# A transformer chain on one core: the projection by tokens made of three rounded products

## The chip, the core and the metric
The kernel runs on one core of a Trainium2 chip. The metric is the time on the device in microseconds (us) of one execution, a median over several. A core has TensorE (matrix products, with weight loads that overlap them), VectorE, ScalarE, GpSimd, and SyncE, which issues most transfers. Products are accumulated in PSUM, in eight banks of 128 partitions by 512 columns of float32.

## The reference, cut to what matters
512 tokens with 1024 channels pass through four layers in float32: two of a first kind (one loop body, run twice), an "even" and an "odd" one. Each begins alike:

```
h = rms_norm(x, pre_mix_w[l])
u = h @ w_in[l]          # then split into parts for convolution, attention, delta rule ...
```

Most columns of `u` are wanted with channels on the partitions. A few are wanted with tokens on the partitions: 408 in each layer of the first kind (the attention's values and the delta rule's gates), 512 in the even layer (half of the gated unit's input), 280 in the odd one (values and gates). Behind come the mixers, an output projection, and a feed-forward (in the odd layer a mixture of experts).

## The kernel before, in words
Activations lie as 8 channel tiles of 128 partitions by 512 tokens (`KD = 8`, `SEQ = 512`, `TT = 4` token tiles). The work is a sequence of phases, written out by hand. `phase` opens semaphores of its own, gives each engine its list of instructions, and closes with a barrier of all engines; nothing crosses it. Every engine works through its list in order and waits only on semaphores.

`rms_norm` leaves the normed stream in `mem.h` and has loaded the weights `w_tm` for the token-major projection; at its end TensorE runs filler products, whose results nobody reads (`fill_in`, L239).

`token_major` (L633) then multiplies: for each token tile and each channel tile the stream's 128 x 128 piece stands in the array and the weights' 408, 512 or 280 columns move (L647). These are products in full float32. ScalarE copies each finished bank out (L660). Beside it `Primer` readies the phase to come: SyncE loads two units of its weights into `weight_ring`, ScalarE rounds the first to `w_high[:, 0]` (L223), VectorE writes the remainder to `w_low[:, 0]` (L230).

`project` (L603) takes SBUF for the parts of its source and calls `linear` (L409), the general dense layer. There a product of float32 matrices is made of three products of rounded parts (type fp32r): high by high, high by low, low by high (L501 to L503). Weights come in units of two output tiles, 16 pieces of 128 x 128, through two slots: load (L472), round on ScalarE (L518), remainder on VectorE (L561), products, copy out (L622). With `source` given, the phase first has to split the stream: ScalarE rounds eight tiles (L554), VectorE takes eight remainders (L597), and TensorE runs five fillers and then, in the first tile of each even unit, waits for the remainders one by one. With `source=None` the parts are there already and there are no fillers. With `primed=SPLIT`, slot 0 is ready: ScalarE and VectorE only mark it so with semaphore increments (VectorE's is L591).

`split_ring` holds `mem.w_high` and `mem.w_low`, 2 slots of 2048 columns. `parts_of` only reserves SBUF. The callers are `second_even`, `second_odd` and `first_block`; in the last two `w_tm` is a buffer of its own.

Of the kernel before, what the change touches and what calls it, by code (L numbers as in the profile page):

```python
# [12 lines left out]
ACT = mybir.ActivationFunctionType  # L13
ALU = mybir.AluOpType
# [3 lines left out]
P = 128  # L18
# [145 lines left out]
@contextmanager  # L164
def phase(nc, *names):


    sems = [nc.alloc_semaphore(f"{n}_{nc.next_id()}") for n in names]
    with nc.Block() as block:
        yield (block, *sems)  # L170
    nc.clear_and_free_semaphores(sems)
    nc.all_engine_barrier()  # L172


@contextmanager
def buffers(nc, **shapes):

    with ExitStack() as stack:
        yield [stack.enter_context(nc.sbuf_tensor(f"{n}_{nc.next_id()}", s, F32)) for n, s in shapes.items()]
# [55 lines left out]
def fill_in(nc, mem, bank, n):  # L235

    tile = mem.filler[:, :]
    for _ in range(n):
        nc.tensor.matmul(bank[:, :], tile, tile.unsqueeze(1).broadcast_to([P, SEQ // P, P]), start=True, stop=True)  # L239
# [363 lines left out]
def project(nc, mem, w, source, evacuate, on_vector=False, primed=0):  # L603

    with parts_of(nc, w.kt) as parts:
        linear(nc, mem, w, parts, evacuate, on_vector, source=source, primed=primed)
# [12 lines left out]
def copy_out(nc, out):  # L619

    def evacuate(bank, tile):
        return nc.scalar.activation(tile_at(out, tile), bank[:, :], ACT.Copy)  # L622
    return evacuate
# [6 lines left out]
    return evacuate  # L630


def token_major(nc, mem, w, cols, source, out, following):  # L633


    with phase(nc, "product", "taken", *Primer.SEMS) as (block, product, taken, *primer_sems):
        primer = Primer(nc, mem, following, primer_sems)

        @block.sync
        def _(sp):  # L640
            primer.load(sp)

        @block.tensor
        def _(pe):
            for t in range(TT):
                for k in range(KD):
                    last = nc.tensor.matmul(mem.bank[t][:, 0:cols], source[:, k, t * P:(t + 1) * P],  # L647
                                            w[:, k * cols:(k + 1) * cols], start=(k == 0), stop=(k == KD - 1))
                last.then_inc(product, 1)

        @block.vector
        def _(dve):
            primer.low(dve)

        @block.scalar
        def _(act):
            primer.high(act)
            for t in range(TT):
                act.wait_ge(product, t + 1)
                nc.scalar.activation(out[:, t, 0:cols], mem.bank[t][:, 0:cols], ACT.Copy).then_inc(taken, 1)  # L660
            act.wait_ge(taken, TT)

class FeedForward:
# [1546 lines left out]
def second_even(nc, mem, a):  # L2212
    with buffers(nc, vec=[P, VECE.size]) as (vec,):
        with buffers(nc, y=[P, KD, SEQ], u=[P, UTE, SEQ], gates=[P, 3, RW_PAIRS, SEQ]) as (y, u, gates):
            decay, rate, gate = [gates[:, i, :, :] for i in range(3)]

            w_tm = gates[:, :, :, :].rearrange("p i j s -> p (i j s)")[:, 0:KD * A_WIDTH]

            pv = y[:, A_GROUPS:KD, :].rearrange("p t n -> p (t n)").rearrange("p (t n) -> p t n", n=A_WIDTH)
            with split_ring(nc, mem):  # L2220
                w_in = Weights(unit_of(a["w_ine"]), UTE // 2, 2, KD)
                rms_norm(nc, mem, mem.x, lambda k: VECE(vec, "norm_mix", k), mem.h,
                         vectors=[(vec[:, :], a["vece"])], ahead=[(w_tm, a["w_tme"])])
                token_major(nc, mem, w_tm, A_WIDTH, mem.h, pv, w_in)
                project(nc, mem, w_in, mem.h, copy_out(nc, u), primed=SPLIT)
            spatial_gate(nc, mem, a, vec, u, pv, y, decay, rate, gate)
            w_out = Weights(unit_of(a["w_oute"]), KD // 2, 2, KD)
            time_mix(nc, mem, vec, u, y, decay, rate, gate, w_out)
            with split_ring(nc, mem):
                project(nc, mem, w_out, y, add_out(nc, mem.x), on_vector=True, primed=LOADED)  # L2230
        ff = FeedForward(unit_of(a["w_ffe"]), unit_of(a["w_downe"]), FFN_T, "silu")
        with split_ring(nc, mem):
            rms_norm(nc, mem, mem.x, lambda k: VECE(vec, "norm_ffn", k), mem.h, following=ff.up[0])
            feed_forward(nc, mem, ff, lambda half: add_out(nc, mem.x), lambda half: True)
# [551 lines left out]
def second_odd(nc, mem, a, out):  # L2786
    with buffers(nc, vec=[P, VECO.size]) as (vec,):
        with buffers(nc, y=[P, KD, SEQ], u=[P, UTO, SEQ], tm=[P, TT, TMO], rope=[P, 2, SEQ], k_cmp=[P, C_KV, N_CMP],
                     v_cmp=[P, C_KV, HEAD]) as (y, u, tm, rope, k_cmp, v_cmp):
            with split_ring(nc, mem):  # L2790
                w_in = Weights(unit_of(a["w_ino"]), UTO // 2, 2, KD)
                with buffers(nc, w_tm=[P, KD * TMO]) as (w_tm,):
                    rms_norm(nc, mem, mem.x, lambda k: VECO(vec, "norm_mix", k), mem.h,
                             vectors=[(vec[:, :], a["veco"])],
                             ahead=[(w_tm[:, :], a["w_tmo"]), (rope[:, :, :], a["rope"])])
                    token_major(nc, mem, w_tm, TMO, mem.h, tm, w_in)
                project(nc, mem, w_in, mem.h, copy_out(nc, u), primed=SPLIT)
            w_out = Weights(unit_of(a["w_outo"]), KD // 2, 2, KD)
            compress(nc, mem, a, vec, rope, u, y, k_cmp, v_cmp, w_out)
            sparse_attention(nc, mem, rope, u, tm, k_cmp, v_cmp, y)  # L2800
            with split_ring(nc, mem):
                project(nc, mem, w_out, y, add_out(nc, mem.x), on_vector=True, primed=LOADED)
        mixture(nc, mem, a, lambda k: VECO(vec, "norm_ffn", k))
        rms_norm(nc, mem, mem.x, lambda k: VECO(vec, "final", k), mem.h, store=out)
# [509 lines left out]
def layer_of(array, l):  # L3314

    one = array[bass.ds(l, 1)]
    names = "abcdefg"[:len(one.shape) - 1]
    return one.rearrange(f"z {' '.join(names)} -> (z {names[0]}) {' '.join(names[1:])}")
# [11 lines left out]
def first_block(nc, mem, a):  # L3330
    with nc.Fori(0, DEPTH) as l, buffers(nc, vec=[P, VEC1.size]) as (vec,):
        with buffers(nc, y=[P, KD, SEQ], u=[P, UT1, SEQ], tm=[P, TT, TM1],
                     lam=[P, 4 * DIFF_DIM + 2], gates=[P, 2, 2 * DELTA_HEADS]) as (y, u, tm, lam, gates):
            with split_ring(nc, mem):
                w_in = Weights(unit_of(a["w_in1"], l), UT1 // 2, 2, KD)
                with buffers(nc, w_tm=[P, KD * TM1]) as (w_tm,):
                    rms_norm(nc, mem, mem.x, lambda k: VEC1(vec, "pre_mix", k), mem.h,
                             vectors=[(vec[:, :], layer_of(a["vec1"], l))],
                             ahead=[(w_tm[:, :], layer_of(a["w_tm1"], l)),
                                    (lam[:, :], a["lam"][bass.ds(l, 1), :].partition_broadcast(P)),  # L3340
                                    (gates[:, :, :], a["gates"][bass.ds(l, 1), :, :].partition_broadcast(P))])
                    token_major(nc, mem, w_tm, TM1, mem.h, tm, w_in)
                project(nc, mem, w_in, mem.h, copy_out(nc, u), primed=SPLIT)
            diff_attention(nc, mem, vec, lam, u, tm, y, a["dist"])
            delta_net(nc, mem, vec, gates, u, tm, y)
            with split_ring(nc, mem):
                w_out = Weights(unit_of(a["w_out1"], l), KD // 2, 2, KD)
                mixer_norms(nc, mem, vec, lam, u, y, w_out)
                project(nc, mem, w_out, y, copy_out(nc, mem.h), primed=SPLIT)
        ff = FeedForward(unit_of(a["w_ff1"], l), unit_of(a["w_ff2"], l), D_FF // P, "relu")  # L3350
        with split_ring(nc, mem):
            add_norm(nc, mem, mem.h, lambda k: VEC1(vec, "post_mix", k), mem.x, lambda k: VEC1(vec, "pre_mlp", k), mem.h,
                     following=ff.up[0])

            feed_forward(nc, mem, ff, lambda half: add_out(nc, mem.h) if half else copy_out(nc, mem.h), bool)
        rms_norm(nc, mem, mem.h, lambda k: VEC1(vec, "post_mlp", k), None, add_to=mem.x)
# [152 lines left out]
```

## Time and profile before

| | us |
|---|---|
| Median of 3 runs (lowest, highest) | 4316.92 (4315.79, 4318.95) |
| Profiled execution, whole | 4322.24 |
| Its span, first to last instruction | 4320.4 |
| TensorE busy (share) | 4047.2 (94%) |
| VectorE busy (share) | 1539.7 (36%) |
| ScalarE busy (share) | 1323.6 (31%) |

The profile comes from one execution. A group of instructions is named by the line that issues it, its engine, and output<-inputs. "PEld" is the weight load of TensorE. Products are pipelined: each lasts longer than the distance to the next, and the distance is the pace. "Idle before" names what let the engine go on. The granted clock (PEclk) is a share of 2.4 GHz; 0.5 is 1.2 GHz. Times in the timeline run from the first instruction.

### The profile page before, as it was taken

The numbers are of one execution on the slowest core, as the hardware profiler recorded it, in microseconds if no ns is written. First come the engines' busy times: TensorE is split into PE (matmuls) and PEld (weight loads), VectorE is DVE, ScalarE is ACT, GpSimd is POOL, SyncE is SP. The second block draws the span as 40 slices with busy tenths as digits, with TensorE's granted clock in tenths as the row PEclk, the third lists the DMA queues.
The fourth block names the chain that finished last, engine by engine and source line by source line (L and its number), as shares of the span: only waits on it lengthen the run. The fifth ranks groups of instructions, "written<-read, shape, count | busy, mean of one in ns | idle before, by whom it ended". The sixth has DMA issues, their size and how long they took to land. (4 is left out here: it accounts for less than half of the span.)

```text
span 4320.4 us, 56641 instructions
## 1 busy us (share of the span) xinstructions
PE 4047.2 (94%) x22051; PEld 3372.8 (78%) x22051; DVE 1539.7 (36%) x2719; ACT 1323.6 (31%) x2282; POOL 224.2 (5%) x187
## 2 busy tenths in 40 slices
PE   8999999999999989999998889999998879999999
PEld 5778787787677878678766776877776659999998
DVE  2364544332226554333333654322315421111121
ACT  2364443232237544332223332322223311111111
POOL 0150100000006010000000000000000000000000
PEclk9998989999999888999999889999999789999999
DMA  3100011221210000122211001222221025555544
GB/s 125 44 1 1 0 39 69 89 96 59 76 53 1 1 0 29 69 88 97 68 69 54 1 1 68 91 89 85 82 73 65 15 72 187 204 212 180 217 169 148
DMA packets 54648, 333.49 MB, mean 77 GB/s; under 512 B 7600, under 2 KB 8496, under 8 KB 23520
## 3 DMA queue, kind: packets, MB, share of 16 engines
q1 hardware_dynamic: 51904, 324.95, 21.5%
q0 software_dynamic: 2592, 6.49, 0.6%
q8 instruction: 99, 1.62, 0.2%
q14 instruction: 53, 0.43, 0.0%
HBM read 326.17 MB, written 4.19 MB: 76 GB/s over the span
## 5 line engine op out<-in xcount | busy, mean ns | idle before, releaser
L501 PE MATMUL bank<-high 128*128 128x512 f32 x2480 | 973.5, 393 | 40.8 <-DVEq L591 22.8
L502 PE MATMUL bank<-low,high 128*128 128x512 f32 x2480 | 972.0, 392 | 0.0
L503 PE MATMUL bank<-high,low 128*128 128x512 f32 x2480 | 972.0, 392 | 0.0
L501 PEld LDWEIGHTS bank<-high 128*128 128x128 f32 x2480 | 470.0, 190 | 146.8 <-DVEq L591 25.7
L503 PEld LDWEIGHTS bank<-high,low 128*128 128x128 f32 x2480 | 469.5, 189 | 98.8
L502 PEld LDWEIGHTS bank<-low,high 128*128 128x128 f32 x2480 | 469.6, 189 | 97.3
L561 DVE TENSOR_TENSOR low<-weight_ring,high 128x2048 fp32r<-128x2048 f32 (+1 forms) x144 | 319.3, 2219 | 544.8 <-ACT high L518 544.8
L3137 PE MATMUL bank<-chosen,glu_ring 128*128 128x176 f32 x2816 | 424.6, 313 | 0.0
L3137 PEld LDWEIGHTS bank<-chosen,glu_ring 128*128 128x128 f32 x2816 | 421.5, 191 | 0.0
L518 ACT ACTIVATE high<-weight_ring 128x2048 fp32r<-128x2048 f32 (+1 forms) x144 | 266.6, 1853 | 262.9 <-PE bank L503 229.1
L239 PE MATMUL bank<-filler 128*128 128x512 f32 x1023 | 291.3, 432 | 20.4 <-PEq L172 14.4
L239 PEld LDWEIGHTS bank<-filler 128*128 128x128 f32 x1023 | 204.5, 203 | 83.4 <-issue 32.9
L3151 PE MATMUL bank<-hidden,down_ring 128*128 128x176 f32 x1408 | 211.3, 313 | 0.0
L3151 PEld LDWEIGHTS bank<-hidden,down_ring 128*128 128x128 f32 x1408 | 210.4, 190 | 0.0
L1414 DVE TENSOR_TENSOR joint<-bank,level_masks 128x512 f32<-128x512 f32 x224 | 153.8, 691 | 145.9 <-PE bank L1433 145.9
L741 POOL TENSOR_TENSOR y<-y,scaled 128x512 f32<-128x512 f32 x120 | 149.6, 1274 | 1007.1 <-ACT scaled L775 1007.1
L3259 DVE TENSOR_TENSOR hidden<-silu,bank 128x176 f32<-128x176 f32 x88 | 29.7, 337 | 385.8 <-ACT silu L3215 385.8
L3215 ACT ACTIVATE silu<-bank 128x176 f32<-128x176 f32 x88 | 27.9, 317 | 448.6 <-PE bank L3137 448.6
L569 DVE TENSOR_TENSOR gated<-gated,bank 128x512 f32<-128x512 f32 x86 | 58.9, 685 | 284.8 <-ACT gated L525 158.5
L622 ACT ACTIVATE u<-bank 128x512 f32 (+1 forms) x84 | 50.3, 598 | 332.0 <-PE bank L503 332.0
L1446 PE MATMUL bank<-weight_ring,joint 128*128 128x128 f32 x1152 | 151.8, 276 | 0.0
L1446 PEld LDWEIGHTS bank<-weight_ring,joint 128*128 128x128 f32 x1152 | 139.5, 192 | 0.9
(506 smaller groups left out, 4653.5 us busy)
## 6 DMA issues: line engine op xcount, KB each, us to landing
glu_ring<-in_w_expert SPq DMA_DIRECT2D x88, 1024.0 KB, 5.1
weight_ring<-in_w_ff SPq DMA_DIRECT2D x64, 1024.0 KB, 5.0
down_ring<-in_w_expert_down SPq DMA_DIRECT2D x64, 704.0 KB, 5.0
weight_ring<-in_w_in SPq DMA_DIRECT2D x22, 1024.0 KB, 4.8
weight_ring<-in_w_ffe SPq DMA_DIRECT2D x22, 1024.0 KB, 4.8
weight_ring<-in_w_downe SPq DMA_DIRECT2D x16, 704.0 KB, 4.1
weight_ring<-in_w_ino SPq DMA_DIRECT2D x11, 1024.0 KB, 4.9
weight_ring<-in_w_ine SPq DMA_DIRECT2D x9, 1024.0 KB, 4.9
```

Source lines behind the costliest of these rows:

```text
L239: nc.tensor.matmul(bank[:, :], tile, tile.unsqueeze(1).broadcast_to([P, SEQ // P, P]), start=True, stop=True)
L501: nc.tensor.matmul(mem.bank[b][:, :], whole, high[:, k, :], start=(k == 0), stop=False)
L502: nc.tensor.matmul(mem.bank[b][:, :], whole, low[:, k, :], start=False, stop=False)
L503: last = nc.tensor.matmul(mem.bank[b][:, :], rest, high[:, k, :], start=False, stop=(k == kt - 1))
L518: nc.scalar.activation(w_high[:, s, :], mem.ring[:, s, 0:size], ACT.Copy).then_inc(high_ready[s], 1)
L561: nc.vector.tensor_tensor(w_low[:, s, :], mem.ring[:, s, 0:size], w_high[:, s, :], ALU.subtract).then_inc(low_ready[s], 1)
L569: nc.vector.tensor_tensor(whole, whole, mem.bank[b][:, :], ALU.mult).then_inc(taken[b], 1)
L741: nc.gpsimd.tensor_tensor(y[:, c, :], y[:, c, :], scaled[:, n % CONV_SLOTS, :], ALU.add).then_inc(added, 1)
L1414: nc.vector.tensor_tensor(chunks(joint[:, n, :]), chunks(turn_bank(i)[:, :]), mask, ALU.mult) \
L1446: last = nc.tensor.matmul(product_bank(i)[:, c], joint[:, n, c], matrix[:, n, c], start=True, stop=True)
L3137: last = nc.tensor.matmul(two(low[s])[:, half, :], glu_ring[:, s, at:at + P], chosen[:, k, :], start=(k == 0), stop=(k == KD - 1))
L3151: last = nc.tensor.matmul(two(high[m // 2])[:, m % 2, :], down_ring[:, s, k * P:(k + 1) * P], hidden[:, k, :], start=(k == 0), stop=(k == ...
```

## The change
`token_major` gets two more buffers, the stream's parts, and makes each product of three rounded ones. The loop over channel tiles is now outermost, the one over token tiles inside: the four token tiles accumulate in banks 0 to 3 side by side, with three products each per channel tile. ScalarE rounds the weights' piece and the stream's tile, VectorE takes both remainders, tile by tile. The weights' parts lie in slot 1 of the ring's parts, free in this phase, in four places of `cols` columns each; for channel tiles 4 to 7 ScalarE waits on `used` until TensorE has left the place. TensorE begins with seven fillers into bank 4.

The stream's parts are reserved by the caller and passed on to `linear` directly, without `source`, so it splits nothing and fills nothing. In `second_odd` and `first_block`, `w_tm` now lies in the memory of `y`, which is written only later.

```diff
-def token_major(nc, mem, w, cols, source, out, following):
+def token_major(nc, mem, w, cols, source, parts, out, following):
+    places = KD // 2
+    w_high, w_low = mem.w_high[:, 1, :], mem.w_low[:, 1, :]
+    high, low = parts
...
+        of = [slice(k * cols, (k + 1) * cols) for k in range(KD)]
+        at = [of[k % places] for k in range(KD)]
...
         @block.tensor
         def _(pe):
-            for t in range(TT):
-                for k in range(KD):
-                    last = nc.tensor.matmul(mem.bank[t][:, 0:cols], source[:, k, t * P:(t + 1) * P],
-                                            w[:, k * cols:(k + 1) * cols], start=(k == 0), stop=(k == KD - 1))
-                last.then_inc(product, 1)
+            fill_in(nc, mem, mem.bank[TT], 7)
+            for k in range(KD):
+                pe.wait_ge(w_low_ready, k + 1)
+                pe.wait_ge(low_ready, k + 1)
+                for t in range(TT):
+                    to, tokens = mem.bank[t][:, 0:cols], slice(t * P, (t + 1) * P)
+                    nc.tensor.matmul(to, high[:, k, tokens], w_high[:, at[k]], start=(k == 0), stop=False)
+                    nc.tensor.matmul(to, high[:, k, tokens], w_low[:, at[k]], start=False, stop=False)
+                    last = nc.tensor.matmul(to, low[:, k, tokens], w_high[:, at[k]], start=False, stop=(k == KD - 1))
+                    if k == KD - 1:
+                        last.then_inc(product, 1)
+                if k < KD - places:
+                    last.then_inc(used, 1)
 
         @block.vector
         def _(dve):
+            for k in range(KD):
+                dve.wait_ge(w_high_ready, k + 1)
+                nc.vector.tensor_tensor(w_low[:, at[k]], w[:, of[k]], w_high[:, at[k]], ALU.subtract) \
+                    .then_inc(w_low_ready, 1)
+                dve.wait_ge(high_ready, k + 1)
+                nc.vector.tensor_tensor(low[:, k, :], source[:, k, :], high[:, k, :], ALU.subtract) \
+                    .then_inc(low_ready, 1)
             primer.low(dve)
 
         @block.scalar
         def _(act):
+            for k in range(KD):
+                if k >= places:
+                    act.wait_ge(used, k - places + 1)
+                nc.scalar.activation(w_high[:, at[k]], w[:, of[k]], ACT.Copy).then_inc(w_high_ready, 1)
+                nc.scalar.activation(high[:, k, :], source[:, k, :], ACT.Copy).then_inc(high_ready, 1)
             primer.high(act)
...
@@ second_odd; first_block and second_even alike @@
-                with buffers(nc, w_tm=[P, KD * TMO]) as (w_tm,):
...
-                    token_major(nc, mem, w_tm, TMO, mem.h, tm, w_in)
-                project(nc, mem, w_in, mem.h, copy_out(nc, u), primed=SPLIT)
+                w_tm = y[:, :, :].rearrange("p t n -> p (t n)")[:, 0:KD * TMO]
...
+                with parts_of(nc, KD) as parts:
+                    token_major(nc, mem, w_tm, TMO, mem.h, parts, tm, w_in)
+                    linear(nc, mem, w_in, parts, copy_out(nc, u), primed=SPLIT)
```

## Rows read from the trace of the kernel before

**Rows 1.** The page, part 1: busy us, share of the span, instructions.
```profile
PE 4047.2 (94%) x22051; PEld 3372.8 (78%) x22051; DVE 1539.7 (36%) x2719; ACT 1323.6 (31%) x2282; POOL 224.2 (5%) x187
```

**Rows 2.** Groups by line and form, TensorE: count, busy us, mean ns, idle before.
```profile
L647 PE MATMUL bank<-w_tm,h_branch 128*128 128x408 f32 x128 | 44.3, 507 | 1.6 <-PEq L172 1.6
...
L647 PE MATMUL bank<-gates,h_branch 128*128 128x512 f32 x64 | 27.7, 593 | 0.8 <-PEq L172 0.8
...
L647 PE MATMUL bank<-w_tm,h_branch 128*128 128x280 f32 x64 | 15.3, 400 | 0.8 <-PEq L172 0.8
```

**Rows 3.** Busy time by stretch: stretch, length, TensorE busy (count), clock, DMA share, GB/s.
```profile
35.00:57.50 22.50, 22.16 (x64) 1.00 0.25 94
...
2216.00:2243.90 27.90, 27.70 (x64) 1.00 0.20 76
3096.60:3112.10 15.50, 15.33 (x64) 1.00 0.37 135
...
60.60:64.40 3.80, 3.76 (x10) 0.55 0.62 252
...
2247.20:2260.00 12.80, 12.80 (x57) 1.00 0.41 152
```

**Rows 4.** Timeline, first layer's seam: start us, us (merged), instruction, idle before.
```profile
58.80 1.40 PE L239 MATMUL bank<-filler 128*128 128x512 f32 x5 [1.44 <-PEq L172]
59.14 4.28 ACT L554 ACTIVATE high<-h_branch 128x512 fp32r<-128x512 f32 x8 [1.23 <-PEq L172]
...
59.80 4.91 DVE L597 TENSOR_TENSOR low<-h_branch,high 128x512 fp32r<-128x512 f32 x8 [15.51 <-ACT high L554]
...
60.64 0.56 PE L501 MATMUL bank<-high 128*128 128x512 f32 x1 [0.45 <-DVE low L597]
```

**Rows 5.** One line's instructions, odd dense layer: ns min/median/max, first to last start.
```profile
L622 ACT ACTIVATE u<-bank x22: 597/599/601, 3121.1 to 3235.2; 128x512 f32 x16, 128x512 f32<-128x512 f32 x6
```

**Rows 6.** Timeline, the first dense layer's rounded products.
```profile
61.42 0.63 PE L503 MATMUL bank<-high,low 128*128 128x512 f32 x1
...
64.36 0.40 PE L501 MATMUL bank<-high 128*128 128x512 f32 x1
...
70.94 0.39 PE L503 MATMUL bank<-high,low 128*128 128x512 f32 x1
```

**Rows 7.** Timeline, odd layer's attention: weight loads of two 128-column rounded products.
```profile
3282.22 0.30 PEld L2586 LDWEIGHTS bank<-masked,exact_ident 128*128 128x128 f32 x2
```

**Rows 8.** Groups by line and form, ScalarE: rounding copies of two widths.
```profile
L518 ACT ACTIVATE high<-weight_ring 128x2048 fp32r<-128x2048 f32 x128 | 244.7, 1912 | 178.9 <-PE bank L503 148.3 <-PEq L172 30.6
...
L518 ACT ACTIVATE high<-weight_ring 128x1408 fp32r<-128x1408 f32 x16 | 21.9, 1383 | 84.0 <-PE bank L503 80.8 <-PEq L172 3.2
```

**Rows 9.** Timeline, first token-major stretch: the next layer's preparation and an evacuation.
```profile
40.06 1.91 ACT L223 ACTIVATE high<-weight_ring 128x2048 fp32r<-128x2048 f32 x1 [12.50 <-DMA weight_ring<-in_w_in]
...
41.87 0.49 ACT L660 ACTIVATE tm<-bank 128x408 f32<-128x408 f32 x1
42.00 2.29 DVE L230 TENSOR_TENSOR low<-weight_ring,high 128x2048 fp32r<-128x2048 f32 x1 [9.02 <-ACT high L223]
```

**Rows 10.** Timeline, a seam without fillers inside the feed-forward, TensorE.
```profile
892.53 0.50 PE L501 MATMUL bank<-high 128*128 128x512 f32 x1 [2.22 <-DVEq L591]
...
894.27 0.63 PE L501 MATMUL bank<-high 128*128 128x512 f32 x1
```

**Rows 11.** One line's instructions: VectorE's mark in the first layer's seam.
```profile
L591 DVEq EVENT_SEMAPHORE  x1: 21/21/21, 58.8 to 58.8; - x1
```

**Rows 12.** Timeline, the even layer's seam, TensorE.
```profile
2245.30 1.39 PE L239 MATMUL bank<-filler 128*128 128x512 f32 x5 [1.52 <-PEq L172]
...
2247.14 0.47 PE L501 MATMUL bank<-high 128*128 128x512 f32 x1 [0.45 <-DVE low L597]
```

**Rows 13.** Groups by line and form: 128-column products, full precision (L830), rounded (L2586).
```profile
L830 PE MATMUL bank<-const_cols,probs 128*128 128x128 f32 x384 | 52.5, 282 | 1.4 <-ACT y L767 1.4
...
L2586 PE MATMUL bank<-masked,exact_ident 128*128 128x128 f32 x64 | 14.8, 315 | 0.0
```

More of the change, by code:

```diff
@@ L630, in add_out @@
     return evacuate
-def token_major(nc, mem, w, cols, source, out, following):
-    with phase(nc, "product", "taken", *Primer.SEMS) as (block, product, taken, *primer_sems):
+def token_major(nc, mem, w, cols, source, parts, out, following):
+    places = KD // 2
+    w_high, w_low = mem.w_high[:, 1, :], mem.w_low[:, 1, :]
+    high, low = parts
+    with phase(nc, "w_high_ready", "w_low_ready", "high_ready", "low_ready", "used", "product", "taken", *Primer.SEMS) as (
+            block, w_high_ready, w_low_ready, high_ready, low_ready, used, product, taken, *primer_sems):
         primer = Primer(nc, mem, following, primer_sems)
+        of = [slice(k * cols, (k + 1) * cols) for k in range(KD)]
+        at = [of[k % places] for k in range(KD)]
         @block.sync
@@ L2223, in second_even @@
                          vectors=[(vec[:, :], a["vece"])], ahead=[(w_tm, a["w_tme"])])
-                token_major(nc, mem, w_tm, A_WIDTH, mem.h, pv, w_in)
-                project(nc, mem, w_in, mem.h, copy_out(nc, u), primed=SPLIT)
+                with parts_of(nc, KD) as parts:
+                    token_major(nc, mem, w_tm, A_WIDTH, mem.h, parts, pv, w_in)
+                    linear(nc, mem, w_in, parts, copy_out(nc, u), primed=SPLIT)
             spatial_gate(nc, mem, a, vec, u, pv, y, decay, rate, gate)
@@ L2791, in second_odd @@
                 w_in = Weights(unit_of(a["w_ino"]), UTO // 2, 2, KD)
-                with buffers(nc, w_tm=[P, KD * TMO]) as (w_tm,):
-                    rms_norm(nc, mem, mem.x, lambda k: VECO(vec, "norm_mix", k), mem.h,
-                             vectors=[(vec[:, :], a["veco"])],
-                             ahead=[(w_tm[:, :], a["w_tmo"]), (rope[:, :, :], a["rope"])])
-                    token_major(nc, mem, w_tm, TMO, mem.h, tm, w_in)
-                project(nc, mem, w_in, mem.h, copy_out(nc, u), primed=SPLIT)
+                w_tm = y[:, :, :].rearrange("p t n -> p (t n)")[:, 0:KD * TMO]
+                rms_norm(nc, mem, mem.x, lambda k: VECO(vec, "norm_mix", k), mem.h,
+                         vectors=[(vec[:, :], a["veco"])],
+                         ahead=[(w_tm, a["w_tmo"]), (rope[:, :, :], a["rope"])])
+                with parts_of(nc, KD) as parts:
+                    token_major(nc, mem, w_tm, TMO, mem.h, parts, tm, w_in)
+                    linear(nc, mem, w_in, parts, copy_out(nc, u), primed=SPLIT)
             w_out = Weights(unit_of(a["w_outo"]), KD // 2, 2, KD)
@@ L3335, in first_block @@
                 w_in = Weights(unit_of(a["w_in1"], l), UT1 // 2, 2, KD)
[L3336 to L3343, printed above, removed]
+                w_tm = y[:, :, :].rearrange("p t n -> p (t n)")[:, 0:KD * TM1]
+                rms_norm(nc, mem, mem.x, lambda k: VEC1(vec, "pre_mix", k), mem.h,
+                         vectors=[(vec[:, :], layer_of(a["vec1"], l))],
+                         ahead=[(w_tm, layer_of(a["w_tm1"], l)),
+                                (lam[:, :], a["lam"][bass.ds(l, 1), :].partition_broadcast(P)),
+                                (gates[:, :, :], a["gates"][bass.ds(l, 1), :, :].partition_broadcast(P))])
+                with parts_of(nc, KD) as parts:
+                    token_major(nc, mem, w_tm, TM1, mem.h, parts, tm, w_in)
+                    linear(nc, mem, w_in, parts, copy_out(nc, u), primed=SPLIT)
             diff_attention(nc, mem, vec, lam, u, tm, y, a["dist"])
```

## The prediction
> **What bounds the kernel now.** I read the page's busy shares first: TensorE is busy 94% of a span of 4320.4 us, VectorE 36%, ScalarE 31% [rows 1]. So only what TensorE executes, or waits for, can move the time. The groups by line and form then give the products that the change rewrites: 64 instructions with 408 moving columns in each of two runs of the layer loop, 64 with 512, 64 with 280 [rows 2]. The busy time by stretch shows each of the four stretches filled to the edge by them (22.16, 22.16, 27.70, 15.33 us, together 87.35) at a granted clock of 1.00, that is 2.4 GHz [rows 3]. Last, the timeline shows the seam behind: last product, a 1.44 us gap, five filler products, and only 1.84 us after the first filler the first real product of the dense layer, let go by VectorE's remainder of the stream [rows 4]. All of this is in series on TensorE. The dense layer behind the seam is bound by TensorE too: in the odd block 22 evacuations start from 3121.1 to 3235.2 us, 5.43 us apart, close to 24 products of 0.227 us [rows 5, 6].
>
> **1. The products.** A full-precision product is two instructions here (32 products, 64 instructions). From 280 to 408 columns the 64 instructions gain 6.83 us [rows 3], so a column costs 0.833 ns in one instruction and 1.67 ns in a product. The rounded products of the dense layers are one instruction each and start 0.227 us apart at 512 columns (64.36 to 70.94 over 29 of them [rows 6]); at 0.833/2 = 0.417 ns a column that is 213.3 ns plus 14 ns. After the change there are 32 x 3 = 96 rounded instructions a stretch. No row shows one with 408 or 280 columns. If the 14 ns stays fixed, they come every 0.184 and 0.131 us; if it is proportional, every 0.181 and 0.124. Above, the bound is 0.227 as for 512 columns (something other than columns sets the pace). Could weight loads do that? Two loads for 128-column rounded products take 0.30 us together where one lasts 0.19, so they start 0.11 apart [rows 7]; that is under 0.131. I take 0.184 and 0.131.
>
> The Trainium skill, page "TensorE: Matmul & The Clock Gate", section "Back-to-back issue gap", gives N/2.4 + 2.5 ns, which is 215.8 ns at 512 columns; this trace shows 227, so for this data type the row decides. By the page's figure the four stretches would be another 4.4 us shorter.
>
> **2. The head.** Real products now wait for ScalarE's rounded weights and stream and VectorE's remainders. The seam shows such a chain: first filler 58.80, ScalarE 59.14, VectorE 59.80, product 60.64, so 1.84 us [rows 4]. The new one has a copy of the weights more ahead of the stream's: eight copies of 512 columns take 4.28 us, 0.52 each in a row [rows 4, 8]; with (1912 - 1383)/640 = 0.83 ns a column [rows 8] 0.44 for 408 and 0.33 for 280. The weights' remainder on VectorE lies beside the stream's copy. The first product thus comes 2.28, 2.36 and 2.17 us in (408, 512, 280). The 7 new fillers need about 6 x 0.23 + 0.39 = 1.8 us and hide in it.
>
> **3. Supply.** Per channel tile ScalarE needs 0.44 + 0.52 = 0.96 us and VectorE at most 0.60 + 0.60 = 1.2 (eight remainders in 4.91 us [rows 4]); TensorE needs 12 x 0.184 = 2.2, 1.57 at 280 columns. From tile 4 on ScalarE waits for a place, free when TensorE leaves tile k - 4; three tiles of products (4.7 us at least) then stand between, against 2 us of preparing. Behind that wait on ScalarE queue the next layer's rounding (1.91 us), VectorE's remainder (2.29) and the four evacuations. The tightest is 280 columns: place for tile 7 free at 2.17 + 4 x 1.57 = 8.5, copies done at 9.4, rounding 11.3, remainder 13.7, products done 14.9. Covered; if it were not, up to 2 us would stand open in this one stretch. The ring's loads are issued at the start as before, and used from 40.06, 4.9 us in, in the first stretch [rows 9]. The tail stays: all four banks now end in the last tile, 3 x 0.184 = 0.55 apart, and an evacuation takes 0.49 [rows 9]; after the last product still one is due.
>
> Stretches, first filler to end of last product (a last product lasts its distance plus 0.17):
> - 408: 2.28 + 95 x 0.184 + 0.35 = 20.1, before 22.16: -2.05, twice.
> - 512: 2.36 + 95 x 0.227 + 0.39 = 24.3, before 27.70: -3.4.
> - 280: 2.17 + 95 x 0.131 + 0.30 = 14.9, before 15.33: -0.4.
> Sum -7.9. With 0.181 and 0.124 it is -9.1; with 0.227 throughout it is +9.6 (24.2 twice, 24.1 once).
>
> **4. The seam.** The dense layer now finds both parts. Its 5 fillers, the 16 copies and remainders, and the wait go. What is late next is the mark from VectorE that slot 0 is ready: in the feed-forward's unfilled seams TensorE is let go by just that mark [rows 10]; in our seams it falls with the first filler, at 58.8 [rows 11]. I allow 0.1 us behind it. So 1.84 becomes 0.1: -1.74 at each of four seams (the others have the same 1.84, as the even block's 2245.30 to 2247.14 [rows 12]), -7.0. At the other end, a gap as long as the 2.22 us of [rows 10] leaves 1.44 + 1.84 - 2.22 = 1.06 a seam, 2.7 us less in all. The slot-1 rounding, queued behind the eight stream copies so far, starts 4.3 us earlier and was hidden (unit 0 takes 10.9 us). The eight waits per even unit on the stream's parts also go; the steady 5.43 us of [rows 5] says they cost nothing. Moving the weights into y's buffer changes an address, no instruction.
>
> **Sum.** -7.9 - 7.0 = -14.9 us against the profiled execution's 4322.24 (span 4320.4 plus 1.84 around it): 4307.3. The median of the runs shown is 5.3 us lower, 4316.92, so I forecast **4302 us**.
>
> **Rivals.**
> (a) The clock. In the first layer TensorE fell to 1.2 GHz right behind the seam: products of 0.63 us instead of 0.39, mean clock 0.55 from 60.6 to 64.4 [rows 3, 6]; in the other three seams, equally built, it stayed at 1.00 (the even block's stands for them [rows 3]). A slow stretch of 3.4 us costs 1.7. The seams without fillers inside the feed-forward, gap 2.22 us, do fall (products of 0.63 us behind it [rows 10]). Ours will have a gap of 1.44 + 0.1 without fillers; the even block's 1.52 gap followed by fillers and another 0.45 wait did not fall [rows 3, 12]. If all four seams fall: +5.1, 4307. If all four heads fall too (gap 0.77, fillers, then half a microsecond of waiting): eight stretches for one, +11.9, 4314.
> The Trainium skill, same page, section "The HAM clock gate (the 'warmup' mystery)", says the throttled state is the default and activity lifts it; that speaks against taking out fillers, and the first seam agrees. By it rival (a) is real.
> (b) The pace does not fall with columns: 0.227 everywhere. Then +9.6 - 7.0 = +2.6: 4320, no change. Against it the 0.11 us between loads and the per-column rows; for it only that no row shows the form.
> (c) The other side: rounded products with fewer columns lose the one-pass rate. The rows give it some colour: a 128-column rounded product (L2586) takes 0.315 us in the mean, a full-precision one of the same size (L830) 0.282 in the mean [rows 13], where 512 columns show 0.39 against 0.59 [rows 2, 6]. If 408 and 280 columns ran at full precision's pace per instruction (0.342, 0.236), the stretches would be 35.3 twice and 25.0: +13.1, +13.1, +9.6, with -3.4 and -7.0: +25.5, 4342. It decides from 0.052 us more for each of the 288 instructions with short rows (14.9/288), 0.236 at 408. I doubt it: those are single pairs among other work, and a duration of 0.17 us plus the 0.11 between their loads [rows 7] gives 0.28 whatever the columns do.
>
> **How the numbers follow.** Forecast with its neighbourhood 0.80, (a) in force 0.10, (b) 0.05, (c) 0.04, else 0.01. The forecast's own range is 4294 to 4308: down by 1.2 for the proportional pace, and by 1.7 for each slow stretch elsewhere (the unfilled feed-forward seams among them) that a program 15 us shorter may not meet; up by one to three slow stretches. For 8 in 10 with part of (a): 4293 to 4312. Some 0.2%, 8.6 us, is what a measurement tells from no change; below 4308.3 is faster. Half of (a) and all of the forecast's case are faster: 0.85; same 0.11 (half of (a), (b)); slower 0.04.
>
> **What would show it.** Right: 96 instructions a stretch, 0.184 and 0.131 us apart at clock 1.00; TensorE busy without gaps behind the first real product, 2.2 to 2.4 us after the first filler; a gap of about 1.55 us at the seam and no L597-like remainder there; stretches of 20.1, 24.3, 14.9. Wrong: a distance of 0.227 at 280 columns (b) or above it (c); distances of 0.43 behind the seams (a); TensorE waiting on VectorE between tiles, which would break step 3.

## The result and the profile after

The changed kernel takes 4288.98 us in the median of 11 runs (4283.1 to 4309.83), the kernel before, run beside it, 4318.17 (4307.16 to 4325.53). The ratio is 0.9938, 95% interval 0.9923 to 0.9952: 26.8 us less. Forecast were 4302 us and a gain of 14.9, with a range of 4293 to 4312. The direction was right, the size was not: nearly twice the gain. Two executions, one of run 1 (6186.64 us) and the profiled one of run 9 (6188.29 us), were in a slower state and are left out of every figure below, so that run 9 has no profile.

The profiled execution took 4308.07 us, 14.2 less than that of before, which looks like the forecast's 14.9. First the page of the changed kernel, then the granted clock of this execution and of a second profiled one of the same kernel.

```profile
span 4306.3 us, 57009 instructions
...
PE 4030.0 (94%) x22187; PEld 3386.2 (79%) x22187; DVE 1556.6 (36%) x2751; ACT 1339.6 (31%) x2314; POOL 224.2 (5%) x187
```

```profile
core 0: 4306.3 us, clock 0.948
```

```profile
core 0: 4283.1 us, clock 0.955
```

The same program, 23 us apart, with the shorter time at the higher clock. So one pair of profiles cannot confirm a total, and what has to be read first is what is the same in both. Busy time by stretch of the changed kernel (stretch, length, TensorE busy and count, clock, DMA share, GB/s): the four token-major stretches and the beginnings of the four dense layers, answering to [rows 3].

```profile
35.50:57.50 22.00, 20.02 (x104) 1.00 0.25 96
1130.90:1152.90 22.00, 19.96 (x103) 1.00 0.25 96
2207.20:2233.50 26.30, 23.90 (x103) 1.00 0.22 80
3080.60:3096.80 16.20, 14.38 (x104) 1.00 0.34 130
57.40:70.00 12.60, 12.56 (x48) 0.86 0.46 168
1152.90:1165.00 12.10, 12.09 (x46) 0.86 0.50 175
2233.50:2246.00 12.50, 12.49 (x55) 1.00 0.51 169
3096.80:3110.00 13.20, 13.20 (x58) 1.00 0.47 160
```

The new products, by line and form, against [rows 2]; then the timeline of the first head (the time from the first filler to the first product) and the first seam, against [rows 4]; then VectorE's mark in that seam, against [rows 11].

```profile
L656 PE MATMUL bank<-high 128*128 128x408 f32 x64 | 22.4, 351 | 0.2
...
L656 PE MATMUL bank<-high 128*128 128x512 f32 x32 | 12.5, 391 | 0.2 <-DVE low L671 0.2
...
L656 PE MATMUL bank<-high 128*128 128x280 f32 x32 | 9.4, 294 | 0.0
```

```profile
35.58 1.83 PE L239 MATMUL bank<-filler 128*128 128x512 f32 x7 [0.77 <-PEq L172]
37.49 0.42 PE L656 MATMUL bank<-high 128*128 128x408 f32 x1
...
55.27 0.35 PE L658 MATMUL bank<-high,low 128*128 128x408 f32 x1
57.44 0.47 PE L501 MATMUL bank<-high 128*128 128x512 f32 x1 [1.82 <-DVEq L591]
...
58.49 0.63 PE L502 MATMUL bank<-low,high 128*128 128x512 f32 x1
```

```profile
L591 DVEq EVENT_SEMAPHORE  x1: 21/21/21, 57.1 to 57.1; - x1
```

TensorE's first product starts 1.91 us after its first filler. It runs 96 products 0.187 us apart without a gap, idles 1.82 us and then finds the dense layer ready. From the first filler or product to the dense layer's first product (called a stage below):

| us | first, l=0 | first, l=1 | even | odd | sum |
|---|---|---|---|---|---|
| before | 25.44 | 25.44 | 31.07 | 18.51 | 100.46 |
| after | 21.86 | 21.86 | 26.17 | 16.08 | 85.97 |
| difference | -3.58 | -3.58 | -4.90 | -2.43 | -14.49 |
| forecast | -3.8 | -3.8 | -5.1 | -2.1 | -14.9 |

The second profile of either kernel repeats these to 0.03 us. Behind the first two seams the clock falls (0.86; products of 0.63 us at 58.49), 1.65 us each. In the first profile of before only the first seam's did, in its second profile the first's and the fourth's.

### The profile page after: what moved, and what is told of

It is laid out like the page before. It is cut to its first block and busy times, and to the rows that moved or that the text cites. A ratio compares the mean times of both kernels' runs of the same rounds, so it can differ in the third digit from the quotient of the medians.

```text
span 4306.3 us, 57009 instructions
## 1 busy us (share of the span) xinstructions
PE 4030.0 (94%) x22187; PEld 3386.2 (79%) x22187; DVE 1556.6 (36%) x2751; ACT 1339.6 (31%) x2314; POOL 224.2 (5%) x187
```

## Where the other half is: the granted clock

Each run lists its mean clock. Through all runs of the full kernels whose clock is listed (172, of twelve kernels, each with a level of its own) one common slope fits to 2.1 us: -3659 us per unit of clock. The last column is each kernel's level, read at a clock of 0.950.

| kernel | runs | mean us | mean clock | us at 0.950 by the fit |
|---|---|---|---|---|
| before | 73 | 4321.6 | 0.9472 | 4311.5 |
| before, as a kernel of its own (run 1) | 11 | 4318.1 | 0.9481 | 4311.1 |
| changed | 11 | 4292.8 | 0.9518 | 4299.4 |
| changed, again (2) | 6 | 4292.1 | 0.9522 | 4300.0 |
| products alone (3) | 12 | 4304.6 | 0.9496 | 4303.1 |
| seam alone (4) | 12 | 4311.3 | 0.9487 | 4306.7 |
| before, 6 fillers (5) | 11 | 4317.0 | 0.9494 | 4314.7 |
| changed, 16 fillers (6) | 5 | 4293.2 | 0.9528 | 4303.4 |
| changed, 10 fillers (7) | 5 | 4295.5 | 0.9512 | 4299.9 |
| changed, odd layer 12 (8) | 10 | 4301.0 | 0.9496 | 4299.5 |
| changed, tail fillers (11) | 5 | 4296.0 | 0.9504 | 4297.4 |
| before, 7 fillers (12) | 11 | 4322.1 | 0.9485 | 4316.4 |

At equal clock the change is worth some 12 us; 0.0046 of clock are another 17. The clock column is rounded to 0.001 (3.7 us), so this is a split, not a measurement of either part. Where the time lies is read from the four profiles of the two kernels, the span cut into five kinds of stretches. A mixer's stretch runs from its first TensorE instruction to the first product of the output projection.

| us | up to the first token-major product or filler | token-major and seam, four | dense layers, four | mixers, four | behind the mixers, four |
|---|---|---|---|---|---|
| before | 35.20 | 100.46 | 474.85 | 1369.41 | 2340.51 |
| before, again | 34.95 | 100.45 | 476.46 | 1377.29 | 2333.65 |
| changed | 35.58 | 85.97 | 476.56 | 1367.39 | 2340.79 |
| changed, again | 35.45 | 85.94 | 476.63 | 1351.72 | 2333.31 |

The 14.5 us are in both pairs. The mixers are 2.0 us shorter in the first pair and 25.6 in the second. What lies behind them differs by 7 us between the two profiles of either kernel. In the changed kernel that is the part behind the odd mixer, where the experts run: 877.9 us in the first profile, of these 54.6 at 1.2 GHz, and 869.9 with 37.6 in the second. That the first pair came so near the forecast was luck.

## Experiments

**1 and 2. Both kernels again.** No edit. 

> The kernel before, once more, for its spread and the clock of every run. Theory A (lottery of the clock): the four seam stretches are steps of fixed length; what else moved is time at 1.2 GHz in the mixers, whose amount is drawn anew in every execution. Then plotted against the granted clock the runs lie on one line, us = a - b x clock, with b near 3400 us per unit (the eleven runs of the changed kernel: 4309.8 at 0.947, 4283.1 at 0.955), and the line of the kernel before lies 14.5 us above that of the changed one. Theory B (another part of the change saves more than the seams show): the distance between the lines is 25 us or more. Median expected 4312 to 4322, profiled clock 0.944 to 0.951.

> The changed kernel once more. Theory A: median 4283 to 4300; where its profile has a granted clock above 0.950 the time missing against the first profile (4306.3) lies in the mixers and in the seams' slow stretches alone, while the four token-major stages stay at 21.9, 21.9, 26.2, 16.1 us. Theory B: some stage other than those is shorter than in both earlier profiles at equal time at 1.2 GHz.


Measured: 4318.6 us (ratio to before 0.9991, 0.9976 to 1.0006), profiled clock 0.947; and 4292.34 (0.994, 0.9927 to 0.9954), 0.955. The lines of the fit lie 12 us apart, not 25, so theory B is out. The 23 us between the changed kernel's two profiles are not in the mixers and seams alone, as expected: 15.7 are in the mixers, 8 behind the odd one. The second pass of the first kind's mixer, in the profiles of before (first execution), before again, changed, changed again:

```profile
1277.84:1720.31 442.47, 409.89 (x2847) 0.89 0.02 7
```

```profile
1276.90:1719.90 443.00, 410.83 (x2846) 0.89 0.02 7
```

```profile
1276.58:1712.19 435.61, 403.28 (x2846) 0.91 0.02 7
```

```profile
1269.40:1704.80 435.40, 402.21 (x2846) 0.91 0.02 7
```

Same instructions, 7 us less, at a higher clock, in both profiles of each kernel. Two against two speaks against a draw by chance (theory A as first put), and the mixer's code is untouched.

**3. Products alone.** The changed kernel, but the dense layer splits its source again:
```diff
-                    linear(nc, mem, w_in, parts, copy_out(nc, u), primed=SPLIT)
+                    linear(nc, mem, w_in, parts, copy_out(nc, u), source=mem.h, primed=SPLIT)
```


> The changed token-major phase, but the dense layer behind it splits the stream itself again with its five fillers. Stages token-major plus seam (first filler or product to the dense layer's first product): 1.73 us longer than in the changed kernel at each of four places, so 23.6, 23.6, 27.9, 17.8 us. Theory A: 6.9 us above the changed kernel at equal clock. If the seam's missing fillers cost slow stretches in the changed kernel (two of four seams show one in its first profile, 1.7 us each), the gap in the median is smaller, about 4 us. Theory B puts the surplus of some 12 us in one of the two parts: this kernel then shows it or not.


Measured: 4302.56 us (0.9964, 0.9951 to 0.9976). Stages 23.36, 23.36, 27.53, 17.59: 8.6 us less than before, and the seam's share is 1.4 to 1.5 a piece, not 1.73. No seam falls in clock. The second mixer takes 435.4 us here.

**4. Seam alone.** Full-precision products, the stream's parts made beside them, tile by tile, on ScalarE (shown) and VectorE; the weights are not split:
```diff
         def _(act):
+            for k in range(KD):
+                nc.scalar.activation(high[:, k, :], source[:, k, :], ACT.Copy).then_inc(high_ready, 1)
             primer.high(act)
```


> The full-precision products and their loop order as before; ScalarE and VectorE make the stream's parts beside them, and the dense layer takes them without fillers. Expected -1.74 us at each of four seams: stages of 23.7, 23.7, 29.3, 16.8 us where the kernel before has 25.44, 25.44, 31.07, 18.51. Theory A: 7.0 us below the kernel before at equal clock. Theory B: one of this and the kernel with the products alone shows some 12 us more than that.


Measured: 4308.98 us (0.9979, 0.9963 to 0.9995). Stages 23.96, 23.95, 29.57, 17.01, -1.5 each, -6.0. No seam falls in clock here either, though none has fillers. The second mixer takes 450.9 us; the profiled execution is the slowest of the twelve. The two halves shorten the stages by 8.6 and 6.0, together 14.6, and by their ratios the whole by 15.6 (10.4 to 21.2) and 9.1 us (2.2 to 16.0). Theory B's single culprit is not there. The surplus of the products' half is clear of noise, that of the seam's half is not.

**A sharper theory.** The clock record of each trace lists when the granted clock changed. Within one execution all falls lie on one regular grid of times, to 0.007 us, in all profiles. Where a kernel starts on it differs from run to run, but the first mixer brings all into step: the output projection behind it started 0.42 to 0.83 us behind a grid point in all twelve profiles, wherever the mixer itself had started (from 0.2 to 3.4). From there the lengths in between set where the second mixer starts. I call the time from the last grid point to a mixer's start its offset. A': the offset decides how much of the mixer runs at 1.2 GHz. B': it does not.

**5 to 8. Moving the offset.** Fillers at the head of the token-major phase:
```diff
+            fill_in(nc, mem, mem.bank[TT], pad)      # before: pad=6 (run 5) or 7 (run 12), first kind only
```
```diff
-            fill_in(nc, mem, mem.bank[TT], 7)        # changed: 16 (run 6), 10 (7) in the first kind, 12 (8) in the odd layer
```


> The kernel before with six fillers put ahead of the token-major products in both layers of the first kind: pure extra work, 1.43 us each, TensorE's stage 25.44 -> 26.9 us. Theory A' (the first mixer brings the program into step with the grid of clock changes; where the second layer's mixer then begins on that grid is set by the lengths in between, and so is its time at 1.2 GHz): offset of the second mixer's start from the last change of the clock goes from 1.4-1.8 us to 2.85-3.2, the changed kernel's 3.1-3.2, and the mixer takes about 435.5 us instead of 442.5-443.0. Net 2.9 - 7: faster than the kernel before by some 4 us in the median, though it only does more. Theory B' (the change itself made the second mixer shorter, through addresses or otherwise; the clock is drawn at random): mixer stays 442 to 443, and the kernel is 2.9 us slower.

> The changed kernel with 16 fillers instead of 7 at the head of the token-major phase in the first kind of layer: the first product comes 3.8 us in instead of 1.91, +1.9 us twice. [...] Theory B': +3.8 us only, the mixer stays at 435.5.

> The changed kernel with 10 fillers at the same place, +0.47 us twice. [...] Theory B': +1 us.

> The changed kernel with 12 fillers instead of 7 in the odd layer's token-major phase alone, +0.94 us once. The odd mixer started at offset 2.46 and 2.84 in the changed kernel's profiles (210.2 and 205.3 us), at 0.04 and 0.08 in two others (221.2, 221.1). Theory A': the offset becomes 3.4 to 0.4 and the mixer 213 to 221 us, +5 to +14 us in the median. Theory B': +0.9 us.


Measured: before with 6 fillers 4316.01 us against 4322.73 in its set, but by the ratio only 2.6 us less (0.9994, 0.998 to 1.0008): the interval holds both forecasts, 4 less and 2.9 more. By the fit the 2.8 us of added work are there (4314.7 against 4311.5 at equal clock) and a higher mean clock gave them back. The changed kernel with 16 took 4295.69 (ratio to before 0.9937), with 10 4298.06 (0.995), with 12 in the odd layer 4300.88 (0.9958), against 4292.34 (0.994) without, from 5, 5 and 10 runs whose standard deviation is 4 to 8 us. The medians decide little, so the profiles have to.

There no forecast of A' for a mixer's length came true. Before with 6 fillers reached offset 2.93 as meant, but its second mixer took 441.4 us, not 435.5. A' put that mixer at 442.5 to 443 us with 16 fillers in the changed kernel and at 451 with 10. But 16 fillers took away the slow stretch behind the second seam (1.65 us), so the offset stayed at 3.17 and the mixer at 435.4; 10 fillers gave 3.40 and 441.1. The odd mixer reached offset 3.41 as meant and took 210.8 us, short of the band of 213 to 221.

**9 and 10. No mixers at all.** In both kernels, all mixers are left out; the output projections of the even and odd layer then load their first weights themselves:
```diff
-            diff_attention(nc, mem, vec, lam, u, tm, y, a["dist"])
-            delta_net(nc, mem, vec, gates, u, tm, y)
+            stand_in(nc, mem, y)        # y = mem.h; the even and odd layers' mixers likewise
```


> The kernel before with the mixers left out (attention, delta rule, gated unit and time mix, sparse attention; a copy of the normed stream stands in for their result), everything else kept. The experts may get other token counts than in the full kernel, so only the difference to the next kernel counts. If the surplus over the seams' 14.5 us comes from time at 1.2 GHz in the mixers, the two differ by 12.8 to 14.5 us (14.5 less up to one slow stretch of 1.7) and the spread of either over its runs is under 3 us where the full kernel's is 6 to 9. If the surplus lies outside the mixers, they differ by 20 us or more.

> The changed kernel with the same mixers left out: 12.8 to 14.5 us below the one before it (theory A'), or 20 us and more (theory B').


Measured: 3134.34 us (3132.03 to 3135.58), and 3117.33 (3116.22 to 3121.64). Difference 17.0 in the median, 15.6 in the mean with a standard error of 1.3: above the forecast's 12.8 to 14.5, but not clearly, and far from the full kernels' 26 to 29. The spread is 4 and 5 us, not under 3, but the full kernels' sets of five or six runs spread by 10 to 19.

**11. Tail fillers.** In the changed kernel, work for TensorE while it waits for the last evacuation and the barrier:
```diff
                 if k < KD - places:
                     last.then_inc(used, 1)
+            fill_in(nc, mem, mem.bank[TT], 3)
```


> The changed kernel with three fillers behind the last product of every token-major phase, where TensorE waits for the last evacuation and the barrier. They take 0.7 us of an idle 1.44 us and should cost nothing. The slow stretches behind the first and second seam go: dense layers 123.7 -> 122.05 us twice, -3.3. Theory A' adds that the second mixer then begins 1.65 us earlier on the grid, at 1.5 instead of 3.1-3.2, where the kernel before had it, and takes 442.5 to 443 instead of 435.5: +3.7 in the median over all. Theory B': -3.3.


Measured: 4293.48 us (0.9936, 0.9917 to 0.9956), the changed kernel's within what 5 runs tell; they cannot tell the two forecasts apart. Timeline of the first and of the second seam, then the clock behind them:

```profile
54.28 0.35 PE L658 MATMUL bank<-high,low 128*128 128x408 f32 x1
54.46 0.87 PE L239 MATMUL bank<-filler 128*128 128x512 f32 x3
56.45 0.48 PE L501 MATMUL bank<-high 128*128 128x512 f32 x1 [1.12 <-DVEq L591]
...
1138.49 0.87 PE L239 MATMUL bank<-filler 128*128 128x512 f32 x3
1140.47 0.47 PE L501 MATMUL bank<-high 128*128 128x512 f32 x1 [1.12 <-DVEq L591]
```

```profile
56.40:69.00 12.60, 12.55 (x55) 1.00 0.46 168
1140.50:1152.50 12.00, 12.00 (x53) 1.00 0.50 176
```

The stages stay at 21.86 us, so the fillers are free, and both slow stretches are gone: dense layers 122.10 and 122.05 instead of 123.7. In the second seam that is the fillers' doing: from the last product's end to the dense layer the gap lies 0.39 to 2.21 us behind a grid point here and 0.44 to 2.26 in the changed kernel, where the clock falls. The first seam proves nothing: the gap begins 1.80 us behind a grid point, and the changed kernel without mixers, whose gap begins at 1.65 without fillers, keeps the full clock there as well.

The second mixer, now at offset 1.38, has the length of the kernel before. Here it is cut in six, first this kernel, then the kernel before (offset 1.42), then the changed one (3.22):

```profile
1262.50:1372.50 110.00, 107.90 (x697) 0.94 0.02 5
1372.50:1422.50 50.00, 43.24 (x275) 0.79 0.00 1
1422.50:1502.50 80.00, 76.47 (x574) 0.90 0.01 1
1502.50:1582.50 80.00, 71.49 (x556) 0.94 0.00 0
1582.50:1662.50 80.00, 72.94 (x550) 0.89 0.00 0
1662.50:1705.30 42.80, 38.86 (x203) 0.76 0.14 51
```

```profile
1276.90:1386.90 110.00, 107.84 (x697) 0.94 0.02 5
1386.90:1436.90 50.00, 43.38 (x275) 0.78 0.01 1
1436.90:1516.90 80.00, 76.25 (x573) 0.90 0.00 1
1516.90:1596.90 80.00, 71.53 (x555) 0.94 0.00 0
1596.90:1676.90 80.00, 72.83 (x551) 0.89 0.00 0
1676.90:1719.70 42.80, 39.02 (x206) 0.76 0.16 53
```

```profile
1269.40:1379.40 110.00, 108.21 (x679) 0.92 0.02 5
1379.40:1429.40 50.00, 43.08 (x308) 0.87 0.00 1
1429.40:1509.40 80.00, 71.53 (x565) 0.95 0.00 1
1509.40:1589.40 80.00, 76.36 (x574) 0.90 0.00 0
1589.40:1669.40 80.00, 71.59 (x556) 0.94 0.00 0
1669.40:1704.80 35.40, 31.43 (x177) 0.81 0.17 63
```

Two different kernels with the same offset agree slice by slice to 0.01 of clock; the same kernel but for three free fillers, with another offset, does not. This is A' at its cleanest, forecast before the run (442.5 to 443; it took 442.8). A rival goes with it: that the second mixer got shorter because the change moved buffers. This kernel has every buffer where the changed one has it. By the fit the tail fillers' kernel is 2.0 to 2.6 us faster at equal clock, and a lower mean clock gives that back.

**12. Seven fillers on the kernel before.**


> The kernel before with seven fillers (six brought the second mixer to offset 2.93 and 441.4 us) ahead of the token-major products in the first kind of layer: +1.66 us twice. Theory A': offset 3.15, mixer 435 to 436 us, net -3.5 on the kernel before. Theory B': +3.3.


Measured: 4324.69 us (0.9995, 0.998 to 1.0009), which again holds both forecasts. Offset 3.18 as meant, mixer 441.4 instead of 435 to 436: its clock falls where those of the other mixers at 3.18 do for 324 us, then one slow stretch lasts longer, and the rest differs. So the offset is not all. The second mixers of the full kernels:

```
offset  0.22   1.38   1.42   1.79   2.90   2.93   3.09   3.17   3.18   3.18   3.22   3.40
us     450.9  442.8  443.0  442.5  432.1  441.4  435.6  435.4  435.4  441.4  435.4  441.1
```
(in this order: seam alone; tail fillers; before again; before; changed, odd 12; before + 6; changed; changed, 16; products; before + 7; changed again; changed, 10.) The kernel before sits in the 442 to 443 group, the changed one in the 432 to 436 group. Neighbours mostly agree, but not always: 2.90 and 2.93 are 9 us apart.

The odd mixer shows the limit more plainly. At offsets of 0.04 (seam alone) and 0.09 (before again) it took 221.2 and 221.1 us, at 0.08 (before + 7) 210.9:

```profile
3231.40:3452.50 221.10, 198.38 (x1065) 0.82 0.10 35
```

```profile
3229.65:3440.60 210.95, 187.89 (x1064) 0.86 0.11 37
```

At 2.46 to 2.49 it took 210.2, 210.2, 204.8 and 209.0 us in four versions of the changed kernel.

**13 to 16. Which mixers.** Both kernels with only the first kind's mixers, and with only the even and odd layers' (the edit of 9, in part).


> The kernel before with the mixers of the even and odd layer left out (a copy of the normed stream stands in) and those of the first kind kept. If the surplus is in the second pass of the first kind's mixer, this kernel and the next differ by 14.5 + 7 = 21 to 24 us, and the profiles show that mixer at 442 to 443 here. If it is elsewhere, by 14 to 17.

> The changed kernel with the even and odd mixers left out: 21 to 24 us below the one before it, its second mixer at 432 to 436 us; or 14 to 17 if the surplus lies in the other mixers.

> The kernel before with only the even and the odd mixer kept. If the surplus is the first kind's, this and the next differ by 14 to 17 us; the odd mixer alone may add up to 8 (mean of profiles 216 against 208 us), then 20 to 24.

> The changed kernel with only the even and the odd mixer kept: 14 to 17 us below the one before it, or 20 to 24 with the odd mixer's share.


Measured: 3958.74 and 3935.95 us, 22.8 apart (21.4 in the mean); 3594.26 and 3570.94, 23.3 apart (23.3). Over the 17.0 (15.6) without mixers that is 5.8 for the first kind's and 6.3 for the others' (5.8 and 7.7 in the means). Added up, 29.1: the full kernels' 26 to 29. Second mixer in the first pair, odd mixer in the second, before and after each:

```profile
1275.90:1722.00 446.10, 412.64 (x2846) 0.89 0.02 7
```

```profile
1271.80:1703.90 432.10, 397.76 (x2846) 0.92 0.02 7
```

```profile
2419.20:2630.50 211.30, 188.47 (x1064) 0.86 0.11 36
```

```profile
2399.20:2604.50 205.30, 181.72 (x1064) 0.90 0.11 37
```

The first line is a miss: 442 to 443 us were expected, and at offset 1.68, between two mixers of that length, it took 446.1. The changed kernel's 432.1 us at 2.87 equals the 432.1 at 2.90 above. Five runs each, with standard errors of 1.7 to 2.3 us: 5.8 and 6.3 have standard errors of some 3 us, so that both groups of mixers have a share is likely and not shown.

## Why the prediction was right or wrong

1. **Products.** Right. 0.187 us apart at 408 columns for 0.184, 0.129 at 280 for 0.131; 280 columns last 0.294 where 0.30 was forecast; clock 1.00. Rivals (b) and (c) are out.
2. **Head.** 1.91 us for 2.28. ScalarE begins with TensorE here (35.55), not 0.34 later as at the seam, whose lag I had taken over. It gave back what the pace cost, which is luck.
3. **Supply.** Right. L656 idles at most 0.2 us in either wide form, over two layers at 408 columns. In the odd layer, the tightest case, the next layer's remainder began at 3091.76 and lasted 2.29 us; the last product began at 3094.80.
4. **Seam.** Gap 1.82 for 1.54 us. VectorE's mark came when it should, 1.46 us behind the last product's end (57.08 in the trace); the first product came 0.36 behind the mark, where I had allowed 0.1. -1.5 us a seam, not -1.74, -6.0 for -7.0. The bound of 2.22 was not reached.
5. **Rival (a).** Real, and small where I put it: two seams fall instead of one, +1.65. Heads never fall. But a missing filler alone does not do it: with the seam alone no seam fell. The tail fillers' run bears the rival out in the second seam. The rule cited from the Trainium skill, page "TensorE: Matmul & The Clock Gate", section "The HAM clock gate (the 'warmup' mystery)", that activity lifts the throttled state, agrees with this seam.
6. **The step that failed** is the clock's term in the forecast's own range: "down ... by 1.7 for each slow stretch elsewhere ... that a program 15 us shorter may not meet". I took the rest of the program's time at 1.2 GHz as given, give or take a stretch or two, and carried the profile's distance to the median over. In its place the mixers, which make up a third of the time and run 40 to 113 us each at 1.2 GHz, lose or gain whole groups of slow stretches when they start elsewhere on the grid. That was worth some 12 us here: 26.8 measured for 14.5 in the stages, and 15.6 without mixers. In the profiles 7 of them are the second mixer's (442.5 and 443.0 us before, 435.6 and 435.4 after). The term's size was unknown, not zero, and the range should have been about 12 us wider on either side; the seam change alone shows in its profile that it can as well go up (450.9).

What is shown: the 14.5 us and their places; that some 12 us more need the mixers; that near offsets gave equal second mixers in two different kernels, and another offset another length. Argued only: that the offset carries the mean difference. It came true in one forecast of a mixer's length out of six, the tail fillers', and near offsets gave unequal mixers in four places at least (2.90 and 2.93, 3.18 twice, 1.68 between 1.42 and 1.79, the odd mixer at 0.04 to 0.09), so there is a second condition that nobody has found. Nearly every kernel has one profile only, and runs of one kernel spread by 10 to 30 us. The odd mixer's 5.5 to 6 us have no test of their own beyond experiment 8.

No version beat the changed kernel by more than the noise. The tail fillers are free and take the slow stretches off the seams, but this program hands the gain back.

## What to carry to other kernels

Count a change by the stages it touches, in the profile: that held to 3% here, in part by luck, as the products gave 8.6 us for 7.9 and the seams 6.0 for 7.0. Where phases at full clock alternate with long phases in which the clock falls again and again (the mixers here: 0.89 to 0.92 in the mean), give the total a second term for the clock, of the size that profiles of one and the same kernel differ by (23 us here), and do not expect it to average out: here it came out one-sided over 11 and 6 runs, probably because the time between two such phases is fixed. Compare profiles stage by stage before explaining a difference of medians, and fit run times against their clock.

## What was not expected of the hardware

- The clock's falls in one execution keep one grid through 4.3 ms (to 0.007 us), and the first mixer, of some 440 us, brings executions that entered it anywhere into step within 0.4 us (offset behind it 0.42 to 0.83 in twelve profiles).
- Three fillers in a gap that exists anyway (0.87 us of 1.99) keep TensorE at 2.4 GHz across the second seam, where it otherwise falls, worth 1.65 us.
- Three rounded products with 280, 408 and 512 columns take 0.39, 0.56 and 0.68 us against 0.47, 0.69 and 0.86 for one of full precision.
